# A hybrid decoder trunk on one core: the 128 x 128 transposes of v and of six heads' outputs taken from TensorE, made of 32 by 32 block transposes on VectorE and transfers inside SBUF

## The reference, cut to what matters

```python
q, f, inp_v, g = jnp.split(h @ w_in, 4, axis=-1)        # h = rms_norm(x); 8 heads of 128 features
q = silu(q);  k = (1 - lb) * sigmoid(-f);  log_f = log(lb + (1 - lb) * sigmoid(f))
# for each chunk of tokens, b = cumsum(log_f):
scores = einsum('bhtk,bhsk,bhtsk->bhts', q, k, exp(b_t - b_s))      # causal
o = scores @ v + (q * exp(b)) @ state
state = exp(b_last) * state + (k * exp(b_last - b)).T @ v
o = rms_norm(o, o_norm_w)                                # per head, over its 128 features
y = (o * silu(g)) @ w_out;   x = x + y
```

## Time and profile before

| what | value |
|---|---|
| median of 3 runs | 1348.18 us (1348.05 to 1348.72) |
| profiled execution, span from the first to the last instruction | 1346.8 us, 1.4 below the median |
| TensorE, busy | 1339.1 us |
| VectorE, busy | 923.1 us |
| ScalarE, busy | 687.2 us |
| GpSimd, busy | 145.3 us |
| granted clock of TensorE, mean | 1.000 |
| chain that ended last | PE 96%, DVE 2%, ACT 1% |

### The profile page before, as it was taken

The page is one execution under the profiler, slowest core; times in us unless marked ns, Lnnn a source line. Parts: engine busy times, 40 slices in busy tenths (PEclk is TensorE's granted clock), DMA queues, the critical chain, the costliest instruction groups (busy, mean ns, idle before and its releaser), DMA issues.

```text
span 1346.8 us, 22178 instructions
## 1 busy us (share of the span) xinstructions
PE 1339.1 (99%) x8759; PEld 1118.0 (83%) x8759; DVE 923.1 (69%) x1659; ACT 687.2 (51%) x1226; POOL 145.3 (11%) x224
## 2 busy tenths in 40 slices
PE   9999999999999999999999999999999999999999
PEld 8888888888888888888888887788888888888887
DVE  7867778564767576666676676865657577777782
ACT  6445555353655565656565656553434335454550
POOL 2422333000000000000000000000000022332220
DMA  6322233423222222222223131332333322232221
GB/s 194 95 80 79 64 94 95 118 79 91 66 79 79 79 79 79 79 79 79 79 68 90 48 92 50 105 93 71 94 94 94 110 76 83 63 93 76 84 64 63
DMA packets 211688, 113.62 MB, mean 84 GB/s; under 512 B 3743, under 2 KB 209889, under 8 KB 211586
## 3 DMA queue, kind: packets, MB, share of 16 engines
q1 hardware_dynamic: 211202, 112.02, 28.9%
q0 software_dynamic: 384, 0.20, 0.1%
HBM read 110.10 MB, written 2.10 MB: 83 GB/s over the span
## 4 chain that ended last, share of the span: by engine, by line
PE 96%; DVE 2%; ACT 1%; issue 1%; DMA 0%; SPq 0%; ACTq 0%; DVEq 0%
PE ps L647 39%; PE ps L662 38%; PE scores L662 4%; PE ps L1088 2%; PE ps L1072 2%; PE ps L1028 2%; PE ps L881 1%; PE scores L1056 1%; PE ps L1056 1%; PE scores L852 1%; PE ps L676 1%; PE ps L883 1%; PE scores L870 1%; PE scores L819 1%; PE ps L892 1%
## 5 line engine op out<-in xcount | busy, mean ns | idle before, releaser
L647 PE MATMUL ps<-op_hi,w_hi 128*128 128x512 f32 (+1 forms) x800 | 311.7, 390 | 0.0
L647 PE MATMUL ps<-op_lo,w_hi 128*128 128x512 f32 (+1 forms) x800 | 305.4, 382 | 0.0
L647 PE MATMUL ps<-op_hi,w_lo 128*128 128x512 f32 (+1 forms) x800 | 304.5, 381 | 0.0
L662 PE MATMUL ps<-w_hi,op_hi 128*128 128x512 f32 (+1 forms) x728 | 294.0, 404 | 1.6 <-DVE op_lo L1844 1.6
L662 PE MATMUL ps<-w_lo,op_hi 128*128 128x512 f32 (+1 forms) x728 | 282.6, 388 | 0.0
L662 PE MATMUL ps<-w_hi,op_lo 128*128 128x512 f32 (+1 forms) x728 | 282.2, 388 | 0.0
L1786 DVE TENSOR_TENSOR w_lo<-raw,w_hi 128x1024 fp32r<-128x1024 f32 x200 | 245.1, 1251 | 12.4 <-ACT w_hi L1274 10.9
L1274 ACT ACTIVATE w_hi<-raw 128x1024 fp32r<-128x1024 f32 x200 | 203.0, 1052 | 26.8 <-PE ps L662 11.2
L647 PEld LDWEIGHTS ps<-op_lo,w_hi 128*128 128x128 f32 x800 | 150.4, 188 | 29.9
L647 PEld LDWEIGHTS ps<-op_hi,w_hi 128*128 128x128 f32 x800 | 150.5, 188 | 27.4 <-DVE op_lo L1829 0.2
L647 PEld LDWEIGHTS ps<-op_hi,w_lo 128*128 128x128 f32 x800 | 150.7, 188 | 27.0
(11 more groups left out here) (228 smaller groups left out, 1944.9 us busy)
## 6 DMA issues: line engine op xcount, KB each, us to landing
raw<-in_b_w_in SPq DMA_DIRECT2D x80, 512.0 KB, 3.9
raw<-in_a_w_in SPq DMA_DIRECT2D x64, 512.0 KB, 4.2
raw<-in_c_w_in SPq DMA_DIRECT2D x24, 512.0 KB, 4.1
raw<-in_a_w_out SPq DMA_DIRECT2D x16, 512.0 KB, 4.3
raw<-in_b_w_out SPq DMA_DIRECT2D x8, 512.0 KB, 4.0
raw<-in_c_w_out SPq DMA_DIRECT2D x8, 512.0 KB, 4.9
xt<-in_x SPq DMA_DIRECT2D x4, 512.0 KB, 6.2
y<-in_norm_w SPq DMA_DIRECT2D x3, 512.0 KB, 4.7
```

The lines of the kernel that those rows point to most:

```text
L647: last = nc.tensor.matmul(bank, a, b, start=(k == 0 and p == 0), stop=(k == KT - 1 and p == 2))
L662: last = nc.tensor.matmul(bank, a, b, start=(k == 0 and p == 0), stop=(k == KT - 1 and p == 2))
```

## The change

For v: VectorE, and no longer ACT, takes v out of its PSUM bank, with a block transpose that turns each 32 by 32 block of the 128 x 512 in place (`turn_v`, ahead of the query levels). SP then moves the blocks to where the full transpose has them: 16 transfers for a head, each of 32 partitions by four pieces of 32 elements (`move_v`), to `a_vt`. They wait for the transpose and for the previous head's values, which read `a_vt`. PE's states wait for their landing. PE's transposes and both of ACT's copies are gone, for all 16 heads.

For the outputs of heads 0 to 5 of each layer: VectorE turns the normed output in blocks, `a_on` to `a_sq` (`turn_o`, in iterations 2 to 7 behind the remainder of chunk 2), SP moves the 16 blocks back to `a_on` (`move_o`), and `into_y` waits for their landing and reads SBUF. ACT's next square, which writes `a_sq`, waits for the same. Heads 6 and 7 keep PE's transposes.

SP's list for the layer is now `load_a`: per iteration chunk 0, chunk 1, the 16 transfers of v, chunk 2, the 16 transfers of the output, chunk 3; the eight chunks of the output weights are the last two rows of it.

```diff
+V_MOVES = 16 * 16
+O_MOVED = HEADS - 2
 # SyncE
+            def move_v(idx, i):
+                head = HEADS * idx + i
+                sp.wait_ge(v_act, head + 1)
+                if head:
+                    sp.wait_ge(o_ready, head)
+                for q in range(4):
+                    rows = slice(q * WINDOW, (q + 1) * WINDOW)
+                    for w in range(WINDOWS):
+                        of = a_v[rows, i % 2].rearrange("a (t w b) -> a w t b", t=TT, w=WINDOWS)[:, w]
+                        sp.dma_start(a_vt[w * WINDOW:(w + 1) * WINDOW, :, rows], of).then_inc(v_landed, 16)
+
+            def move_o(idx, i):
+                sp.wait_ge(o_turned, i - 1 + O_MOVED * idx)
+                for w in range(WINDOWS):
+                    rows = slice(w * WINDOW, (w + 1) * WINDOW)
+                    for q in range(4):
+                        feats = slice(q * WINDOW, (q + 1) * WINDOW)
+                        sp.dma_start(a_on[feats, :, rows], a_sq[rows, :, feats]).then_inc(o_landed, 16)
+
+            def load_a(n, w, w_out):
+                idx = n // 3
+                for r in range(HEADS + 2):
+                    for c, part in enumerate(A_PARTS):
+                        if r >= HEADS:
+                            load_columns(OUT0[n] + (r - HEADS) * 4 + c, w_out, [((r - HEADS) * 4 + c) * P])
+                        elif r or c >= (RAW if n else 2):
+                            load_columns(IN0[n] + r * 4 + c, w, [part * D + r * P])
+                        if c == 1 and r >= 2:
+                            move_v(idx, r - 2)
+                        if c == 2 and 3 <= r <= HEADS:
+                            move_o(idx, r - 1)
...
 # TensorE
                     def states():
                         pe.wait_ge(kT_done, h + 1)
-                        pe.wait_ge(vT_done, h + 1)
+                        pe.wait_ge(v_landed, V_MOVES * (h + 1))
...
-                        turn_v()
...
-                        steps[17] = [turn_v, turn_k]
-                        steps[20] = [turn_o, states] if end else [states]
+                        steps[17] = [turn_k]
+                        steps[20] = [states]
 # ScalarE: v_out and the copy of v to a_v are gone; ahead of the square
+                        if proj and end:
+                            act.wait_ge(o_landed, V_MOVES * (i - 1 + O_MOVED * idx))
 # VectorE
+                    def turn_v():
+                        dve.wait_ge(acc_ready, i * 4 + (A0 + 3))
+                        if i + H0 > 1:
+                            dve.wait_ge(v_landed, V_MOVES * (i + H0 - 1))
+                        nc.vector.transpose(a_v[:, par], acc[0][:]).then_inc(v_act, 1)
...
+                    def turn_o():
+                        dve.wait_ge(on_done, h)
+                        nc.vector.transpose(a_sq.rearrange("p t c -> p (t c)"),
+                                            a_on.rearrange("p t c -> p (t c)")).then_inc(o_turned, 1)
+
                     def into_y():
-                        dve.wait_ge(oT_ready, h)
-                        nc.vector.scalar_tensor_tensor(y[:, i - 2], turn[1][:], vec[:, 16 + idx:17 + idx],
+                        if proj:
+                            dve.wait_ge(o_landed, V_MOVES * (i - 1 + O_MOVED * idx))
+                            of = a_on.rearrange("p t c -> p (t c)")
+                        else:
+                            dve.wait_ge(oT_ready, 2 * idx + i - HEADS + 1)
+                            of = turn[1][:]
+                        nc.vector.scalar_tensor_tensor(y[:, i - 2], of, vec[:, 16 + idx:17 + idx],
...
                     if proj:
                         split_lo_chunk(IN0[n], len(A_PARTS), j, par, 2, ring)
+                        if end:
+                            turn_o()
...
                             split_lo_chunk(IN0[n], len(A_PARTS), j if par == 0 else j + 1, 1 - par, c, a_ring)
+                    turn_v()
                     move_queries(0, a_q[:, par], head, par, 0)
```

More of the change, by code:

```diff
@@ L324, in build @@
         gate_done = sem("gate_done")
-        vT_ready = sem("vT_ready")
-        vT_done = sem("vT_done")
+        v_landed = sem("v_landed")
+        o_turned = sem("o_turned")
+        o_landed = sem("o_landed")
         g_ready = sem("g_ready")
@@ L550, in _ @@
                 if n % 3 == 0:
-                    load_layer(n, a_w_in[n // 3], A_PARTS)
+                    load_a(n, a_w_in[n // 3], w_out)
                 if n == 1:
@@ L563, in _ @@
                                  [part * D + g * P for g in range(HEADS) for part in (0, 2)])
-                load_columns(OUT0[n], w_out, [c * P for c in range(OUT_CHUNKS)])
+                if n % 3:
+                    load_columns(OUT0[n], w_out, [c * P for c in range(OUT_CHUNKS)])
             pieces = [(t, slice(0, D), FINAL[t]) for t in range(TT - 1)]
@@ L800, in body @@
                     later = not static(h) or h > H0
[L802 to L809, removed]
                     def own_and_pairs():
@@ L1394, in body @@
                         gate_sigmoid()
[L1396 to L1401, removed]
                     def k_out():
@@ L1439, in body @@
                     if mix and not proj:
-                        v_out()
                         freed_y(0, 1, 2)
@@ L1487, in body @@
                         split_out(n, (2,))
[L1488 to L1491, removed]
-                        nc.scalar.activation(a_v[:, par], acc[0][:], ACT.Copy).then_inc(v_act, 1)
                     if last_proj:
@@ L1912, in layer_a @@
             def layer_a(n, idx):
-                H0 = HEADS * idx
+                H0, A0 = HEADS * idx, ACC0[n]
                 nc.vector.memset(a_ones, 1.0)
@@ L2071, in o_norm @@
                         dve.wait_ge(rs_done, of + 1)
-                        if not static(of) or of > H0:
-                            dve.wait_ge(oT_ready, of)
+                        if of == H0 + HEADS - 1:
+                            dve.wait_ge(oT_ready, 2 * idx + 1)
                         nc.vector.tensor_tensor(a_on, obank[:].rearrange("p (t c) -> p t c", t=TT),
```

## The result

The changed kernel takes 1358.01 us (median of 4 runs, 1356.24 to 1359.24), the kernel before 1348.45 on the same chip: ratio 1.0069, 95% interval 1.0057 to 1.0081. It is slower by 9.6 us, outside the predicted range on the side that the range left out; 1338.7 was forecast. The profiled execution has a span of 1354.9 us, which is 17.6 above the 1337.3 predicted for it.

The account below looks back on a forecast made before the run. TensorE (PE), busy 1339.1 of 1346.8 us, was taken as the bound. Removed transposes save 12.3 us, layer ends lose 2.8: span 1337.3, plus 1.4 for the median gives 1338.7 us; range 1335.5 to 1344.5.

Parts of the forecast that it names:

- What PE loses: On PE, 28 groups of four transposes go at 0.44 us each: 12.3 us less, middle iterations 26.3 us.
- VectorE's transposes: Block transposes of v and outputs on VectorE, 0.61 us each, hidden in middle iterations by its 3.28 us wait.
- What SP's queue gains: SP's 32 added transfers an iteration at 0.41 us take 13.1 of 26.3 us: not the bound, all landing in time.
- far bound of 2.35: Upper limit in us for one SP issue, from the longest issue seen, when the queue was full.
- the threshold: SP's output transfers reach y in time until an issue costs 0.75 us.
- rival C: SP's queue becomes the bound, longer than PE's iteration above 0.77 us an issue: 1387 to about 1528 us; chance 0.10.
- VectorE waits for landings ahead of y: Listed sign of a wrong forecast: VectorE held before y by moved outputs; 5 us of slack was claimed there.
- The end of each layer: Iterations 7 and 8: VectorE's added transpose makes ACT's keys late, PE stands still 1.4 us a layer, 2.8 for both.
- A: Rival: VectorE's operations at a layer's end shrink and PE loses nothing there, 1335.9 us; chance 0.12.
- B: Rival: small delays in middle iterations, and as much again at the ends, cost 5 us, 1343.7 us; chance 0.11.
- fixed cost of a DMA: For SP's transfers: about 2.0 us each, 64 us an iteration if serial; taken as mostly completion that can overlap.
- The sum: Whole kernel: 12.3 - 2.8 = 9.5 us off the 1346.8 us span gives 1337.3; with 1.4 for the median, 1338.7.

Follow-up runs that it names:

- through HBM: Changed kernel, but each turned tile is stored to an HBM buffer and brought back in 4 transfers, result kept: 1342.8 us, ratio 0.9959.
- six and five: As through HBM, but only six heads' v and five outputs a layer moved, the others on TensorE as before: 1339.08 us, ratio 0.9929.
- the circle cut: Changed kernel with one edit, VectorE's product into y issued behind the turn of v instead of ahead of it: 1346.11 us, ratio 0.9984.
- four transfers a move: Changed kernel, but each move is 4 transfers of 128 rows by 512 B, blocks not put in place (different result): 1342.05 us, ratio 0.9948.

## Why the prediction was wrong

**What PE loses: right.** 0.44 us a group holds in every run: 26.3 us an iteration with both groups gone, 26.74 with one, and 22 x 0.44 = 9.7 us against 9.5 measured (1348.6 - 1339.08).

**VectorE's transposes: right.** 0.70 and 0.71 us, adding 0.63 to its run, where I took 0.61. In the middle they are hidden, as forecast (the wait before the masks is 1.74 us through HBM, about 2 was forecast).

**What SP's queue gains: wrong, and this step turned the sign.** Two faults met. The first is a size: 0.41 us for an issue, with 0.48 as the near bound, came from loads from HBM. For these transfers it is 0.60, and 0.64 from start to start. The far bound of 2.35 covered it, but I gave the stretch from 0.48 up to 0.75 no weight, as all of it counted as safe. The second is the threshold itself, and it was an error of my own sum, not a gap in the trace. "(192.4 - 178.3 - 2)/16 = 0.75 us" starts the output's issues at 178.3, when the output is turned. But v's 16 and a load stand in the same queue from 170; they are done by 178.3 only up to 0.49 us an issue. Above that both moves count: 170 + 32 p + 0.5 + 2 <= 192.4 gives p = 0.62. The measured 0.64 (0.69 in the mean) is just above. That an output is late by a little is not yet the loss, and rival C's reason for one, a queue longer than PE's iteration from 0.77 us an issue, did not arise: what sets the time is the circle, because the turn of v, which starts the next one, stands on VectorE behind the product into y that ends this one. The prediction laid the path out straight and never followed the late instruction's successors on VectorE back to SP. It had even listed "VectorE waits for landings ahead of y" as the sign of being wrong.

**The end of each layer: right in kind, too small, and at the wrong place.** I put the first stop of PE at the output transposes of head 6, 1.4 us in all. The first to be late is the low half of y at the output projection's first matmul, and that had a slack of only 0.2 us before. I had followed VectorE's run of the earlier trace rows to its end and not looked up what it releases in its middle. The runs with a fast middle show PE's wait there alone: 1.9 us a layer with both turns, 1.6 with the eighth v but not the sixth output, 0.6 to 0.8 with the sixth output but not the eighth v, 0.3 with the seventh v, none with six and five. On it came 1.3 more in the changed kernel, with VectorE's 3.18 us wait for the sixth output's landing. That is not the circle alone: with the circle cut the first layer still has a wait of 1.93 us for this landing and the same 3.19 of PE. Behind it came 1.6 of half clock. PE's waits for the low halves sum to 7.9 us, 1.6 of them as before, and the half clock adds 3.2, so 9.5 us stand where the forecast had 2.8. The term mis-sized here is the 1.4 us a layer.

**The rivals.** A (the ends hide it) is refuted by every run with the end's turns moved. B (small delays) comes near the run through HBM, 1342.8, by luck: it put most of its delays in the middle iterations, where that run has none, and its 5 us do not follow from its own terms (0.44 in five iterations of two layers is 4.4 us, with as much again 8.8). C had the right sign and the right place, and the wrong condition. The Trainium skill's fixed cost of a DMA of about 2.0 us ("DMA: Bandwidth & Descriptors", section Anatomy of one DMA) is given there for DMAs that GpSimd issues, which the prediction left out. For these, issued by SP, a delay of that size was seen, a median of 1.9 us from issue to landing, and it was a delay and not a price in the queue, as weighed.

**The sum.** The prediction added 1.4 us to the span for the median; in every run here the launch is 1.8 to 2.0 us longer than its span. That is some 0.4 us of the 19.3 missed.

## What to carry to other kernels

Price a DMA issue by a row with the same source, destination and shape, not by its queue alone, and where there is no such row, take a weight for every value between the bounds. When a threshold for a queue is worked out, start the clock at the first thing that stands in the queue, and then ask of each wait you add whether what is queued behind it feeds the same queue: if so, it is a circle, and its length is compared with the iteration. Here putting one instruction behind another cut it, and leaving the last heads, where VectorE had no slack, as they were gave the rest: 1339.1 to 1339.3 us, 0.7% under the kernel before.

## What the hardware showed that was not expected

- An issue on SP of a transfer from SBUF to SBUF takes 0.60 us, from HBM to SBUF a median of 0.43 (0.32 to 0.56) for the same 16 blocks, from SBUF to HBM 0.60, from ACT's queue (SBUF to SBUF) 0.62; piece size from 128 B to 2 KB changes the SBUF to SBUF issue by less than 0.05. A store of 128 rows of 2 KB to HBM takes 0.35.
- PE's clock after a wait. Granted to the matmuls behind these waits, all at the same place of the program, was sometimes 1.2 GHz, seen as a start every 0.43 us, for some 3 us, and sometimes 2.4 GHz throughout. One case, in the fourth layer of the run with four transfers a move (PE in order of time, then a window of 1290 to 1296, where the last but two column is the granted clock):

```profile
1288.62 0.47 PE L693 MATMUL ps<-w_hi,op_hi 128*128 128x512 f32 x1 [1.94 <-DVE op_lo L1853]
...
1290.66 0.63 PE L693 MATMUL ps<-w_hi,op_hi 128*128 128x512 f32 x1
1291.08 0.63 PE L693 MATMUL ps<-w_hi,op_lo 128*128 128x512 f32 x1
...
1293.58 0.39 PE L693 MATMUL ps<-w_hi,op_lo 128*128 128x512 f32 x1
```

```profile
1290.00:1296.00 6.00, 6.00 (x21) 4.74 (x20) 5.83 (x18) 2.80 (x8) 0.00 (x0) 0.72 0.22 63
```

It fell behind waits of 3.19 (three times), 1.96, 1.94 and 1.61 us, the last three all in the fourth layer, and not behind 2.11, 1.94, 1.88, 1.65, 1.64 and 1.62, two of them in the fourth layer too. So the length of the wait alone does not decide; what else does is left open. It differs between executions of one kernel too: of the ten with the circle cut, the three with a mean granted clock of 0.996 took 1348.2 to 1349.1 us, the four with 0.998 or 0.999 took 1344.1 to 1345.8.
